# A two-layer decoder trunk on one core: the sparse attention's indexer products in groups of four heads, spread over half chunks of the projection before it

## The reference, cut to what matters

```python
def dsa_mixer(q, k, v, iq, ik, iw, tab):
    k_top = min(IDX_TOPK_MAX, S // 4)                      # 128
    def block(qi, qb, iqb, iwb):                           # 128 queries
        idx_logit = jax.nn.relu(jnp.einsum('bthd,bsd->bths', iqb, ik))   # 8 heads of 32
        idx_score = jnp.einsum('bth,bths->bts', iwb, idx_logit)
        idx_score = jnp.where(key_pos[None, :] <= t[:, None], idx_score, NEG_INF)
        _, sel = lax.top_k(idx_score, k_top)
```

## Time and profile before

| | us |
|---|---|
| median of 3 runs (lowest, highest) | 2361.34 (2357.35, 2361.94) |
| the profiled execution, own time | 2359.32 |
| its span, first to last instruction | 2357.2 |
| PE busy (share of the span) | 2245.7 (95%) |
| DVE busy | 1231.7 (52%) |
| POOL busy | 1358.3 (58%) |
| ACT busy | 542.4 (23%) |
| mean granted TensorE clock, of full speed | 0.979 |

### The profile page before, as it was taken

The page is one execution under the profiler, slowest core; times in us unless marked ns, Lnnn a source line. Parts: engine busy times, 40 slices in busy tenths (PEclk is TensorE's granted clock), DMA queues, the critical chain, the costliest instruction groups (busy, mean ns, idle before and its releaser), DMA issues.

```text
span 2357.2 us, 32909 instructions
## 1 busy us (share of the span) xinstructions
PE 2245.7 (95%) x11594; PEld 1895.7 (80%) x11598; DVE 1231.7 (52%) x2377; ACT 542.4 (23%) x1313; POOL 1358.3 (58%) x843
## 2 busy tenths in 40 slices
PE   6999999898989899999999999999989989999997
PEld 5888888687878798888888888888767879888886
DVE  5544324678876556553246445124477655745323
ACT  2111003216751441010031000013256144111000
POOL 5666665471147457666667666666330745766662
PEclk9999999799999999999999999999989999999998
DMA  5433332220023113333323333333211321333331
GB/s 193 166 98 98 90 98 73 103 72 19 24 78 115 54 53 109 98 96 93 98 80 99 98 98 89 95 93 103 68 39 38 108 63 46 109 96 97 91 99 52
DMA packets 62145, 205.60 MB, mean 87 GB/s; under 512 B 6815, under 2 KB 9247, under 8 KB 61652
## 3 DMA queue, kind: packets, MB, share of 16 engines
q1 hardware_dynamic: 55312, 187.86, 26.5%
q10 hardware_dynamic: 6724, 16.29, 2.0%
HBM read 201.98 MB, written 8.70 MB: 89 GB/s over the span
## 4 chain that ended last, share of the span: by engine, by line
PE 86%; DVE 7%; ACT 2%; issue 2%; POOL 1%; DMA 0%; another core or an unknown queue 0%; SPq 0%; ACTq 0%; POOLq 0%; DVEq 0%
PE bank L735 26%; PE bank L737 25%; PE bank L736 25%; PE bank L1004 3%; PE bank L987 2%; PE bank L973 1%; DVE h_lo L1609 1%; POOL sq_sum L629 1%; DVE ev_logit L1796 1%; PE bank L1054 1%; PE bank L763 1%; DVE bank L1670 1%; PE bank L787 1%; DVE od_logit L1796 1%; PE bank L970 1%
## 5 line engine op out<-in xcount | busy, mean ns | idle before, releaser
L605 POOL TENSOR_TENSOR w_lo<-w_raw,w_hi 128x1024 fp32r<-128x1024 f32 (+1 forms) x358 | 866.1, 2419 | 29.9
L735 PE MATMUL bank<-h_hi,w_hi 128*128 128x512 f32 (+1 forms) x2136 | 803.6, 376 | 28.3 <-DVE h_lo L1609 11.6
L736 PE MATMUL bank<-h_lo,w_hi 128*128 128x512 f32 (+1 forms) x2136 | 796.9, 373 | 0.0
L737 PE MATMUL bank<-h_hi,w_lo 128*128 128x512 f32 (+1 forms) x2136 | 796.7, 373 | 0.0
L603 POOL TENSOR_SCALAR w_hi<-w_raw 128x1024 fp32r<-128x1024 f32 (+1 forms) x358 | 382.7, 1069 | 709.4 <-PE bank L737 563.0
L735 PEld LDWEIGHTS bank<-h_hi,w_hi 128*128 128x128 f32 x2136 | 407.9, 191 | 105.9 <-issue 14.8
L737 PEld LDWEIGHTS bank<-h_hi,w_lo 128*128 128x128 f32 x2136 | 407.5, 191 | 70.0
L736 PEld LDWEIGHTS bank<-h_lo,w_hi 128*128 128x128 f32 x2136 | 408.2, 191 | 67.9
L735 PE MATMUL bank<-act_hi,w_hi 128*128 128x512 f32 (+1 forms) x792 | 290.1, 366 | 0.0
L736 PE MATMUL bank<-act_lo,w_hi 128*128 128x512 f32 (+1 forms) x792 | 289.4, 365 | 0.0
L737 PE MATMUL bank<-act_hi,w_lo 128*128 128x512 f32 (+1 forms) x792 | 289.4, 365 | 0.0
(11 more groups left out here) (264 smaller groups left out, 2416.9 us busy)
## 6 DMA issues: line engine op xcount, KB each, us to landing
w_raw<-in_w_up SPq DMA_DIRECT2D x176, 512.0 KB, 3.6
w_raw<-in_w_down SPq DMA_DIRECT2D x64, 448.0 KB, 3.3
w_raw<-in_w_down SPq DMA_DIRECT2D x32, 512.0 KB, 3.5
w_raw<-in_w_ev_in SPq DMA_DIRECT2D x19, 512.0 KB, 3.6
w_raw<-in_w_xkv SPq DMA_DIRECT2D x16, 512.0 KB, 3.6
w_raw<-in_w_od_in SPq DMA_DIRECT2D x16, 512.0 KB, 3.6
bias_line_rows<-bias_lines ACTq DMA_DIRECT2D x1, 6400.0 KB
ev_strip<-bias_line_rows ACTq DMA_DIRECT2D x16, 256.0 KB, 3.0
```

What stands on the lines that cost most here:

```text
L605: pool.tensor_tensor(w_lo[j][:, 0:cols], raw[j][:, 0:cols], w_hi[j][:, 0:cols].bitcast(F32), ALU.subtract).then_inc(split_done, 1)
L735: pe.matmul(out, w_hi[j][:, w], hi, start=first, stop=False)
L736: pe.matmul(out, w_hi[j][:, w], lo, start=False, stop=False)
L737: return pe.matmul(out, w_lo[j][:, w], hi, start=False, stop=last)
```

## The change

PE does the indexer's products in six groups of four heads (`index_logits`), each head of a group in rows of its own of the array and in a bank of its own (banks 4 to 7). Chunks 5 to 8 are cut into halves of four tiles (`half_chunk`): the first half of chunk 5 stands before the transposes of VG, its second half behind them, and one half of chunks 6 to 8 behind each group. There are four `relu` buffers in place of two. Scores lie in the old VG chunk and in two buffers of the norms, so no longer under the key tiles. DVE lets chunks 5, 6 and 7 leave at the start of each query tile, 8 before the rounds, and then one in every second round; three memsets come earlier. POOL makes `cmp_x` two instructions at a time behind the splits of units 15 to 18, and all key low parts and that of KB; ACT rounds the keys as soon as their chunks are there.

```diff
--- before.py
+++ after.py
+IDX_RING = 4
+K_ORDER = (0, 2, 1, 3)
...
-    relu = [n.put(f"relu{j}", [P, T], F32) for j in range(2)]
-    score = [n.put(f"score{j}", [P, T], F32) for j in range(3)]
+    relu = [n.put(f"relu{j}", [P, T], F32) for j in range(IDX_RING)]
+    score = [ev[:, VG, :], sq[0][:], sq_sum[:]]
...
-            def q_parts():
-
-                pool.wait_ge(relu_done, (NT - 1) * IDX_HEADS)
-                pool.wait_ge(rows_done, V_ROWS["vg"] + 1)
-                for k in range(A_HEADS + B_HEADS):
+            def q_parts(k0, k1):
+
+                if k0 == 0:
+                    pool.wait_ge(relu_done, (NT - 1) * IDX_HEADS)
+                    pool.wait_ge(rows_done, V_ROWS["vg"] + 1)
+                for k in range(k0, k1):
                     src, hi, lo = q_head(k)
+                    if k == 3:
+                        pool.wait_ge(mask_done, 1)
...
+            def cmp_tokens(n):
+
+                if n == 0:
+                    pool.wait_ge(chunk_out, CHUNK["ev_in"] + VCMP + 1)
+                    pool.wait_ge(aux_in, AUX["ev"])
...
+                pool.tensor_tensor(cmp_x[DH * odd:DH * odd + DH, kv, :, g, :], blocks, pe_, ALU.add).then_inc(cmp_x_done, 1)
+                pool.wait_ge(cmp_x_done, n + 1)
             def k_low():
 
-                pool.wait_ge(k_hi_done, 2)
-                for half in range(2):
-                    pool.tensor_tensor(k_st[0][1][DH * half:DH * half + DH, :], k_rows(0), k_st[0][0][0:DH, :].bitcast(F32),
-                                       ALU.subtract).then_inc(k_lo_pool, 1)
-                    pool.wait_ge(k_lo_pool, half + 1)
+                for k, n in enumerate(K_ORDER):
+                    pool.wait_ge(k_hi_done, 2 * n + 2)
+                    e = slice(DH * (n % 2), DH * (n % 2) + DH)
+                    for half in range(2):
+                        pool.tensor_tensor(k_st[n][1][DH * half:DH * half + DH, :], k_rows(n),
+                                           k_st[n][0][e, :].bitcast(F32), ALU.subtract).then_inc(k_lo_pool, 1)
+                        pool.wait_ge(k_lo_pool, 2 * k + half + 1)
+
+            def kb_low():
+
+                pool.wait_ge(k_hi_done, 9)
+                pool.tensor_tensor(k_st[4][1][:], ev[:, KB, :], k_st[4][0][:].bitcast(F32), ALU.subtract).then_inc(k_lo_pool, 1)
+                pool.wait_ge(k_lo_pool, 9)
+
+            def even_projection():
+
+                for k in range(R):
+                    straight(UNIT["ev_in"] + k)
+                pre_norm_halves(1)
+                for k in range(R, EV_IN):
+                    straight(UNIT["ev_in"] + k)
+                    if k >= EV_IN - 4:
+                        pool.wait_ge(split_done, UNIT["ev_in"] + k + 1)
+                        cmp_tokens(2 * (k - EV_IN + 4))
+                        cmp_tokens(2 * (k - EV_IN + 4) + 1)
 
             ffn(0, 0)
-            projection("ev_in", EV_IN, 1)
-            cmp_tokens()
+            even_projection()
             k_low()
-            q_parts()
+            q_parts(0, 2)
+            kb_low()
+            q_parts(2, A_HEADS + B_HEADS)
...
                     if phase == 0 and JOBS[0][s][2] == 0 and JOBS[0][s][0] in ("slc", "dsa"):
                         pe.wait_ge(q_lo_done, info["strip"] + 1)
-                    if phase == 0 and s in (2, 3, 4):
-                        pe.wait_ge(k_lo_done, 2 * (s - 1))
+                    if phase == 0 and s in (1, 2, 3, 4):
+                        pe.wait_ge(k_lo_pool, 2 * s)
                     if phase == 0 and JOBS[0][s] == ("dsa", 0, 0):
-                        pe.wait_ge(k_lo_done, 7)
+                        pe.wait_ge(k_lo_pool, 9)
...
+                def half_chunk(c, part):
+
+                    u, b = UNIT["ev_in"] + c, c0 + c
+                    if part == 0:
+                        pe.wait_ge(split_done, u + 1)
+                        pe.wait_ge(chunk_out, b - R + 1)
+                    for k in range(4 * part, 4 * part + 4):
+                        mm = product(b % R, u % R, k, h_hi[:, k, :], h_lo[:, k, :], k == 0, k == KC - 1)
+                    if part:
+                        mm.then_inc(unit_done, 1)
+
+                def index_logits(n):
+
+                    i, first = 1 + n // 2, 4 * (n % 2)
+                    if n:
+                        pe.wait_ge(relu_done, 4 * n)
+                    for j in range(4):
+                        e = slice(IDX_DH * j, IDX_DH * j + IDX_DH)
+                        pe.matmul(bank[4 + j][:, 0:P * (i + 1)], ev[e, IQ + first // 4, P * i:P * i + P],
+                                  ev[e, IK, 0:P * (i + 1)], start=True, stop=True).then_inc(idx_done, 1)
+
+                half_chunk(R + 1, 0)
                 pe.wait_ge(chunk_out, c0 + R + 1)
                 turn_rows("vg", 0, ev[:, VG, :], NT)
-                banks = (B_STAT, B_RT, B_T[(TURN["vg"] + 1) % 2])
-                for k in range((NT - 1) * IDX_HEADS):
-                    i, h = 1 + k // IDX_HEADS, k % IDX_HEADS
-                    e = IDX_DH * (h % 4)
-                    if k >= 3:
-                        pe.wait_ge(relu_done, k - 2)
-                    pe.matmul(bank[banks[k % 3]][:, 0:P * (i + 1)], ev[e:e + IDX_DH, IQ + h // 4, P * i:P * i + P],
-                              ev[e:e + IDX_DH, IK, 0:P * (i + 1)], start=True, stop=True).then_inc(idx_done, 1)
-                chunks("ev_in", EV_IN - 2, R + 1, h_hi, h_lo)
+                half_chunk(R + 1, 1)
+                pe.wait_ge(rows_done, V_ROWS["vg"] + 1)
+                for n in range(6):
+                    index_logits(n)
+                    half_chunk(R + 2 + n // 2, n % 2)
+                chunks("ev_in", EV_IN - 2, R + 5, h_hi, h_lo)
...
-                pe.wait_ge(k_lo_pool, 2)
...
-                    if k >= 2:
-                        act.wait_ge(idx_added, k - 1)
-                    act.activation(relu[k % 2][:, 0:P * (i + 1)], bank[banks[k % 3]][:, 0:P * (i + 1)],
+                    if k >= IDX_RING:
+                        act.wait_ge(idx_added, k - IDX_RING + 1)
+                    act.activation(relu[k % IDX_RING][:, 0:P * (i + 1)], bank[4 + k % 4][:, 0:P * (i + 1)],
                                    ACT.Relu).then_inc(relu_done, 1)
...
+                act.wait_ge(chunk_out, c0 + KW + 1)
+                k_high(2)
+                k_high(3)
+                act.wait_ge(cmp_x_done, 8)
+                act.activation(k_st[4][0][:], ev[:, KB, :], ACT.Copy).then_inc(k_hi_done, 1)
...
-                act.wait_ge(mask_done, NT - 1)
-                k_high(2)
-                k_high(3)
...
+                for tile in (kc, vc, cmp_prob):
+                    dve.memset(tile[:], 0.0).then_inc(cmp_zero, 1)
...
+                    if k % 8 == 0:
+                        leave_next()
                     dve.wait_ge(relu_done, k + 1)
                     if h:
                         dve.wait_ge(idx_added, k)
-                    dve.scalar_tensor_tensor(sc, relu[k % 2][:, 0:w], ev_v[:, 2, i, 88 + h:89 + h],
+                    dve.scalar_tensor_tensor(sc, relu[k % IDX_RING][:, 0:w], ev_v[:, 2, i, 88 + h:89 + h],
                                              sc if h else ev_causal[:, off:off + w], ALU.mult,
                                              ALU.add).then_inc(idx_added, 1)
                 dve.wait_ge(idx_added, (NT - 1) * IDX_HEADS)
+                leave_next()
                 dve.memset(v_pad[2][0][:, :, DH:P], 0.0).then_inc(pad_zero, 1)
-                dve.memset(kc[:], 0.0).then_inc(cmp_zero, 1)
-                dve.memset(vc[:], 0.0).then_inc(cmp_zero, 1)
-                dve.memset(cmp_prob[:], 0.0).then_inc(cmp_zero, 1)
...
-                    if k % 3 != 2:
+                    if k % 2:
...
-                def k_low(n):
-                    dve.wait_ge(k_hi_done, {1: 4, 2: 7, 3: 9}[n])
-                    e = slice(DH * (n % 2), DH * (n % 2) + DH)
-                    for half in range(2):
-                        dve.tensor_tensor(k_st[n][1][DH * half:DH * half + DH, :], k_rows(n),
-                                          k_st[n][0][e, :].bitcast(F32), ALU.subtract).then_inc(k_lo_done, 1)
-
-                def kb_low():
-                    dve.tensor_tensor(k_st[4][1][:], ev[:, KB, :], k_st[4][0][:].bitcast(F32), ALU.subtract).then_inc(k_lo_done, 1)
-
-                attention(0, {0: lambda: k_low(2), 1: lambda: k_low(1), 2: lambda: k_low(3), 6: kb_low})
+                attention(0)
```

More of the change, by code:

```diff
@@ L326, in build @@
     k_lo_pool = sem("k_lo_pool")
-    k_lo_done = sem("k_lo_done")
     q_hi_done = sem("q_hi_done")
@@ L674, in q_parts @@
                     pool.wait_ge(q_lo_done, k + 1)
-            def cmp_tokens():
-                pool.wait_ge(chunk_out, CHUNK["ev_in"] + VCMP + 1)
-                pool.wait_ge(aux_in, AUX["ev"])
-                n = 0
-                for kv, src in enumerate((KCMP, VCMP)):
-                    for g in range(2):
-                        e = slice(DH * g, DH * g + DH)
```

(29 more changed lines are left out.)

## The result

| | before | after |
|---|---|---|
| median, us (lowest, highest; runs) | 2359.35 (2355.21, 2361.94; 4) | 2338.45 (2331.97, 2340.21; 4) |
| ratio of the runs, 95% interval | | 0.9904 [0.9883, 0.9925] |
| profiled execution, own time, us | 2359.32 | 2340.13 |
| its span | 2357.2 | 2338.2 |
| mean granted TensorE clock | 0.979 | 0.980 |

What follows compares the result with a forecast made beforehand. PE's products were taken as the bound nearly everywhere. Terms -20.0 (attention's start), -3.8 (keys) and -0.5 (clock) sum to -24.3, from 2359.3 to 2335.0, moved half way towards the median to 2336; range 2330 to 2347.

Steps and rivals of the forecast that it cites:

- Chunk 8's end, 19.5 earlier: On PE in layer 0's mixer: with groups between half chunks, chunk 8 ends at 452.9 in place of 472.4.
- my estimate of 2.0: On PE: ten more changes of tiling mode at 0.2 us each, about that much taken as already in the group prices.
- C: Rival: PE's clock falls in the indexer's groups and returns behind them, up to +21 us, 2356; chance 0.07.
- D: Rival: the clock stays down beyond the groups, a chunk costing 4.8 more, slower than before, 2404 at all ten; chance 0.03.
- DVE: Additions, with 8.0 of port waits beside splits, end at 459.0 with chunk 8's leave; rounds, leaves and masks end at 514.6.
- The sum only 0.5 less: Without port waits DVE would be 8 us earlier but the total only 0.5 less, since PE is the bound then.
- PE behind chunk 8: Eight chunks, transposes, compressed products and two chunks bring PE to 514.1; attention begins at 515.0 against 534.97, -20.0.
- The tie I forecast: Before the attention, DVE's chain (514.6) and PE's end (514.1) come within 0.5 us of each other.
- The attention's first jobs: -3.8 and -0.5: Waits for key low parts go (-4.2), pipeline filling costs +0.4, together -3.8; a shorter half clock gives -0.5.
- A: Rival: additions pace the groups, splits holding the port for their full 3.4 each; attention about 5.6 later, 2341; chance 0.14.
- B: Rival: the heads of a group don't overlap, 1.7 to 3.3 a group, PE 6 to 9 later, 2344; chance 0.06.
- the half step up from 2335.0 to 2336: The summed time stood 2.0 under the median of the runs, so the forecast number was moved half way.

Runs made afterwards that it cites:

- row: Against the changed kernel: the six groups one after another, no half chunks between them, chunks 6 to 8 behind the last group; median 2347.57 us.
- tiny_splits: Against the changed kernel: GpSimd splits only 2 of the 1024 columns of units 9 to 12; median 2332.83 us.
- same_rows: Against the changed kernel: all four heads of a group use rows 0 to 31 of the array; median 2344.01 us.
- leaves: Against the changed kernel: chunks leave behind two of every three rounds in place of every second; median 2338.11 us.

## Why the prediction was right, point by point

- **Chunk 8's end, 19.5 earlier.** Measured 19.0: from the leave of chunk 4 to VS's transposes, eight chunks behind, it is 92.18 before (516.27) and 73.15 after (497.89). Against the 452.9 of the forecast it is 0.8 late. Groups of 0.73, 0.95 and 1.16 came at 0.71, 0.93 and 1.14, and the waits for ReLUs at 1.03 for 0.8. What I undersized is the change between group and half chunk: from 430.54 to 434.13 are 3.59, less 0.71 leaves 2.88 for a half chunk that I took as 2.72. That is 0.16 a group, 1.0 in six, half of my estimate of 2.0, and I was wrong to take it as contained in the prices. Whether it is the drain at a change of tiling mode (the Trainium skill, TensorEngine Tiling (Array Packing), Key Properties) is shown in part at most: the last product before a group is followed after 0.32 and the one before the transposes, without a change of mode, after 0.23; but the first product behind a group is followed after 0.34, and the first behind the transposes after 0.31 as well.
- **Clock.** It stayed at 1.00 through groups and chunks; rivals C and D did not come. row shows how C would have looked.
- **DVE.** First addition 432.57 against 431.8 (0.65 of it the later chunk 4). Blocked additions lost 8.8 to the splits by their lengths (2.04 for 0.48, 2.70 for 0.75, and five more), forecast 8.0. 16 rounds with 8 leaves took 52.1, forecast 52.2; masks 1.84 for 2.2.
- **"The sum only 0.5 less"** without the port waits was the weakest step: tiny_splits shows 2.4 at the attention's start. The late additions reach PE twice, by the 1.03 before the sixth group and by the 1.11 for VW, whose leave stands behind the rounds. I had priced both waits and yet not ascribed them to the port.
- **PE behind chunk 8.** Wait for VW 1.11 (forecast 1.0), from chunk 16 to chunk 17 6.78 (6.7), two chunks 11.0 (10.9). Two small slips stand in the forecast: 6.7 less 1.09 and plus 1.0 from 496.4 gives 503.0 and not 503.2, and 10.79 for 47 products is 5.5 a chunk and not 5.44. Start -19.0 for -20.0: of the missing 1.0, 0.8 is there at chunk 8, mostly from the 0.16 a group. The tie I forecast was PE's by 0.86.
- **The attention's first jobs: -3.8 and -0.5.** Measured -4.3 from start to end, by two errors that cancel. The filling cost 1.2 (0.99 and 0.18), not 0.4, since nothing covers the first exponential now. The half clock shrank from 10 us to 6 and so gave more than 0.5, some 1.3 by the remainder, an estimate. That the sum of the two came so close is luck.
- **GpSimd.** `cmp_x` was done at 496.9 (forecast 495), the keys at 507.7, KB's low part at 513.2, before 516.6. POOL in order of time:

```profile
496.96 10.76 POOL L700 TENSOR_TENSOR k_st<-ev_proj,k_st 64x512 fp32r<-64x512 f32 x8
...
511.95 1.29 POOL L707 TENSOR_TENSOR k_st<-ev_proj,k_st 128x512 fp32r<-128x512 f32 x1
```

  I had priced KB's low part at 2.4 by the `w_lo` row, which has 1024 columns; with 512 it costs what 64 rows cost, 1.3. The slack hid the error.
- **Rivals.** A: the port waits came at my size, not at 3.4 each, and PE kept the end. B fell by the group prices, and same_rows prices it at 12 and not at 6 to 9.
- **The sum.** The -24.3 came as -23.3 at the attention's end, but as -20.9 at the medians and as -19.2 between the profiled executions. In the traces the difference arose in layer 1's mixer, for which the prediction had no term, and its cause stays open (above); the half step up from 2335.0 to 2336 was meant for another reason, and that it helped is luck.

## What to carry to other kernels

A round of small products that passes between three engines costs PE twice, by its waits and by the clock behind them; cut it into groups (of four here, one bank a head; other sizes were not run), give each product of a group its own rows of the array, and lay between the groups enough large products to cover what ACT and DVE need for one. With both engines nearly full, the order in which a chunk leaves is a price of its own: a leave must stand late enough that its chunk is ready and early enough that nobody waits, so look at both queues before moving it. And judge such a stage by landmarks in the trace, since whole executions scatter by more than most of these effects.

## What was not expected of the hardware

- **One program, two clocks.** One program gave 0.93 and 0.97 over the same 260 us in two executions that had agreed to 0.1 us at the attention's end; from there to the last instruction they differ by 7.3.
- **Busy is not enough for the clock.** In same_rows PE read busy for 4.00 of 4.00 us and the clock fell to 0.59; with the same columns in four row groups it stayed at 1.00. But in same_rows too it was back at 1.00 from 454 to 470, beside the longest groups, and no run shows why it fell where it did.
- **Masks beside GpSimd.** With one SBUF input each they took 0.89, 0.35 and 0.84 in the changed kernel, the first beside KB's low part and the third beside the high part of a query head on GpSimd, and 0.28, 0.35 and 0.42 in leaves, where GpSimd was idle for the first two, and its high part of a query head, which met the third, took 0.94 in place of 0.62. By the Trainium skill (SBUF — State Buffer, SBUF: two separate sides) VectorE also takes the shared port with one input, in a fast mode that uses two ports; these lengths agree with that, though the mode itself is in no trace. I had counted on it for two inputs only. MAX8 takes 0.42, 0.54 and 0.68 in both.
